# A ring of weights and its rounded copies, each 64 bytes off its former place modulo 128, in a split-fp32 transformer kernel

## What is computed

```
x = layer_norm(ALPHA * x + h, ...)
x = layer_norm(ALPHA * x + memory_cross_attention(x, mem, ...), ...)
x = layer_norm(ALPHA * x + conv_glu(x, ...), ...)
```

## The kernel before

| tile | lies on | start in bytes | modulo 128 |
|---|---|---|---|
| ring, w_lo | ring | 16512 | 0 |
| x_lo | tri | 80512 | 0 |
| s_lo | xt2 | 57472 | 0 |
| arena, h_hi, h_lo, m_hi, m_lo, s_hi, w_half, w_swo, yT | arena | 114624 and on | 64 |
| x_hi | arena + 4 x 18432 | 188352 | 64 |
| w_hi | arena + 4 x 20480 | 196544 | 64 |
| xlat, sc_in, small | own | 106432, 105280, 102336 | 64 |

## Time and profile before

### The profile page before, as it was taken

How to read it: one execution, slowest core, us unless ns; L and a number is a source line. 1 busy time by engine, 2 the same in 40 slices (tenths; PEclk the granted TensorE clock), 3 DMA queues, 4 the chain that set the end, 5 groups by cost and what they waited for, 6 DMA issues and landing times.

```text
span 2034.1 us, 33951 instructions
## 1 busy us (share of the span) xinstructions
PE 1919.6 (94%) x13633; PEld 1703.3 (84%) x13633; DVE 1077.8 (53%) x1502; ACT 996.0 (49%) x1703; POOL 1255.3 (62%) x585
## 2 busy tenths in 40 slices
PE   7989999999999989999998899999889999999997
PEld 7889798987999966879987787877679988959996
DVE  5472246633610073135557645688539943947971
ACT  4654345543444362436653444478645545535542
POOL 8758466687888503648896334100569886318995
PEclk9999999999999999999999899999999999988999
DMA  7335377774555534435552222344345554224552
GB/s 263 144 126 206 104 274 304 306 273 166 187 188 187 194 139 163 187 145 186 187 195 100 83 83 83 127 164 166 106 153 186 186 186 148 102 83 172 189 186 103
DMA packets 49218, 342.32 MB, mean 168 GB/s; under 512 B 5264, under 2 KB 7312, under 8 KB 8144
## 3 DMA queue, kind: packets, MB, share of 16 engines
q1 hardware_dynamic: 47440, 331.02, 45.1%
q0 software_dynamic: 1664, 9.70, 1.3%
HBM read 339.65 MB, written 1.05 MB: 167 GB/s over the span
## 4 chain that ended last, share of the span: by engine, by line
PE 73%; DVE 10%; POOL 6%; ACT 6%; issue 4%; DMA 1%; DVEq 0%; POOLq 0%; SPq 0%; ACTq 0%
PE bank L1831 13%; PE bank L1774 11%; PE bank L1768 11%; PE bank L1771 11%; POOL w_lo L2339 4%; PE bank L1881 3%; PE bank L1811 2%; PE bank L1809 2%; PE bank L1806 2%; PE bank L1353 2%; PE bank L1355 2%; PE bank L1356 2%; PE bank L1587 2%; DVE arena L765 2%; ACT arena L1181 1%
## 5 line engine op out<-in xcount | busy, mean ns | idle before, releaser
L2339 POOL TENSOR_TENSOR w_lo<-ring,w_hi 128x1024 fp32r<-128x1024 f32 x404 | 983.7, 2462 | 299.6 <-ACT w_hi L2949 281.4
L1768 PE MATMUL bank<-x_hi,w_hi 128*128 128x256 f32 x2176 | 613.9, 282 | 16.4 <-POOL w_lo L2339 13.0
L1774 PE MATMUL bank<-x_lo,w_hi 128*128 128x256 f32 x2176 | 619.1, 284 | 0.0
L2949 ACT ACTIVATE w_hi<-ring 128x1024 fp32r<-128x1024 f32 x448 | 448.8, 1052 | 293.4 <-DMA ring<-slabs_dram 284.1
L1771 PE MATMUL bank<-x_hi,w_lo 128*128 128x256 f32 x1824 | 511.5, 280 | 0.0
L1768 PEld LDWEIGHTS bank<-x_hi,w_hi 128*128 128x128 f32 x2176 | 414.6, 191 | 27.2 <-issue 27.2
L1774 PEld LDWEIGHTS bank<-x_lo,w_hi 128*128 128x128 f32 x2176 | 413.9, 190 | 0.0
L1771 PEld LDWEIGHTS bank<-x_hi,w_lo 128*128 128x128 f32 x1824 | 348.1, 191 | 0.0
L2871 ACT ACTIVATE arena<-bank 128x512 f32<-128x512 f32 (+1 forms) x179 | 98.3, 562 | 278.8 <-PE bank L1774 190.1
L458 POOL TENSOR_TENSOR w_lo<-ring,w_half 128x1024 fp32r<-128x1024 f32 x32 | 78.1, 2444 | 113.3 <-ACT w_half L1069 113.3
L2339 POOL TENSOR_TENSOR w_hi<-ring,w_hi 128x1024 fp32r<-128x1024 f32 x44 | 104.4, 2395 | 47.9 <-ACT w_hi L2949 47.9
(11 more groups left out here) (365 smaller groups left out, 3685.0 us busy)
## 6 DMA issues: line engine op xcount, KB each, us to landing
ring<-slabs_dram SPq DMA_DIRECT2D x308, 1024.0 KB, 4.8
lnrow<-ln_dram POOLq DMA_DIRECT2D x6, 1024.0 KB, 6.5
arena<-slabs_dram SPq DMA_DIRECT2D x4, 1024.0 KB, 8.0
xt<-xT_dram SPq DMA_DIRECT2D x1, 1024.0 KB, 5.7
xt<-memT_dram SPq DMA_DIRECT2D x1, 1024.0 KB, 11.8
x<-x_dram SPq DMA_DIRECT2D x1, 1024.0 KB, 13.6
arena<-ctx_dram POOLq DMA_DIRECT2D x1, 1024.0 KB, 7.1
lnrow<-ln_dram POOLq DMA_DIRECT2D x2, 512.0 KB, 4.7
```

Of the source, the lines that this page charges most:

```text
L1768: ins = pe.matmul(dst, wh[:, k, c], src[0][:, k, :], start=(k == 0 and (ch == 0 or not both)), stop=False, skip_group_check=both)
L1774: ins = pe.matmul(dst, wh[:, k, c], src[1][:, k, :], start=False, stop=(k == KC - 1), skip_group_check=both)
L2339: pool.tensor_tensor(dst[:, c], ring[:, s, c], w_hi[:, s, c].bitcast(F32), ALU.subtract).then_inc(S["lo_ready"], 1)
L2949: a.activation(w_hi[:, g % RING, c], ring[:, g % RING, c], ACT.Copy) \
```

## The change

Only declarations change. `tri`, `x` and `pt` come ahead of `ring`, `small` moves behind `arena` and is 16 elements shorter, `arena` is 16 elements longer, and `w_hi` starts 20496 elements into it instead of 20480. Three small tiles inside `small` move, one of them (`dcol`) onto `nmx`. The list of instructions of each engine, with its waits, is the same before and after.

```
+        tri_at = aligned()
+        tri = sb("tri", [P, 4, NT, T])
+        x = sb("x", [P, NT, D])
+        pt = sb("pt", [P, NPT])
         ring_at = aligned()
         ring = sb("ring", [P, RING, SLAB])
-        x = sb("x", [P, NT, D])
         xt2_at = aligned()
         xt2 = sb("xt2", [P, KC, 2 * T])
...
-        tri_at = aligned()
-        tri = sb("tri", [P, 4, NT, T])
         lnrow = sb("lnrow", [P, 2, D])
-        pt = sb("pt", [P, NPT])
         row = sb("row", [P, NROW])
-        small = sb("small", [P, 544])
...
-        arena = sb("arena", [P, 28672])
+        arena = sb("arena", [P, 28688])
+        small = sb("small", [P, 528])
...
-        pick = small[:, 256:288]
+        pick = small[:, 232:264]
...
-        dcol = small[:, 232:248]
+        dcol = small[:, 56:72]
...
-        w_hi = part("w_hi", arena_at + 4 * 20480, RING, SLAB)
+        w_hi = part("w_hi", arena_at + 4 * 20496, RING, SLAB)
```

More of the change, by code:

```diff
@@ L221, in aligned @@
             return -(-nc.sbuf_base // 32) * 32
+        tri_at = aligned()
+        tri = sb("tri", [P, 4, NT, T])
+        x = sb("x", [P, NT, D])
+        pt = sb("pt", [P, NPT])
         ring_at = aligned()
         ring = sb("ring", [P, RING, SLAB])
-        x = sb("x", [P, NT, D])
         xt2_at = aligned()
         xt2 = sb("xt2", [P, KC, 2 * T])
-        xT = xt2[:, :, T:2 * T]
-        sideT = xt2[:, :, 0:T]
         ident = sb("ident", [P, P])
@@ L243, in build @@
         arena_at = aligned()
-        arena = sb("arena", [P, 28672])
+        arena = sb("arena", [P, 28688])
+        small = sb("small", [P, 528])
+        xT = xt2[:, :, T:2 * T]
+        sideT = xt2[:, :, 0:T]
         def cut(at, *dims):
@@ L270, in build @@
         half16 = small[:, 136:152]
-        pick = small[:, 256:288]
+        pick = small[:, 232:264]
         modA = small[:, 168:184]
-        lamp = small[:, 288:416]
-        dtn = small[:, 288:544].rearrange("p (t h) -> p t h", t=4)
+        lamp = small[:, 264:392]
+        dtn = small[:, 264:520].rearrange("p (t h) -> p t h", t=4)
         sub_col = small[:, 230:231]
```

## The result

| | before | after |
|---|---|---|
| runs (median) | 2033.4 to 2035.92 us (2034.2, six runs) | 2041.6 to 2044.91 us (2042.56, six runs) |
| ratio of the medians, 95% interval | | 1.0043, 1.0033 to 1.0053 |
| profiled execution, span | 2036.21, 2034.1 us | 2042.38, 2040.3 us |
| granted clock | 0.974 | 0.976 |

The change costs 8.4 us.

The account below looks back on a forecast made before the run. The prediction took TensorE's pace, how fast matmuls follow each other, to bound the kernel. Its terms, +12.2 us for T on x against smaller gains, summed to +0.5 us: 2034.6 us against the median of 2034.16, range 2027 to 2041 us.

Parts of the forecast that it names:

- rival 4: Loads or GpSimd's remainders slow down at the new places and TensorE waits: 5 us or more; chance 0.04.
- T on x: Three-matmul split products on x outside net f0, 1824 triples: 53 steps for 52, 6.67 ns each, +12.2 us.
- One rule fits all five: At 256 columns, moving operand and next stationary operand: 18 steps of 6.67 ns if address / 64 has like parity, 17 if unlike.
- T in f0: The same form T in net f0, its remainder in a slot of w_hi, 352 triples: 52 steps for 53, -2.3 us.
- T on m: Form T with operand m, 8 slabs, 128 triples: two unlike pairs for one, -0.9 us.
- N on m: Form N, with w_hi and w_lo moving, on m, 128 triples: two unlike pairs for one, -0.9 us.
- R on h: 512-column matmuls in groups of six on h, 176 groups: 206 steps for 208, -2.3 us; bounds 0 and -4.7.
- N on x: Form N on x, 256 triples: 51 steps for 54, -5.1 us; bounds -3.4 us (52 steps) and -10.2 us (48).
- Form H: Triples of 512-column matmuls; s_lo and w_lo both move, three like-parity pairs as before: 0 us.
- swo: 8 slabs, 32 groups using w_swo and yT: six like-parity pairs for four, 210 steps for 208, +0.4 us.
- R on x: 512-column groups of six on x, 48 groups: -0.6 us, bounds 0 and -1.6; 3 steps of its old pace unexplained.
- Rival 1: TensorE pays in form T, N on x gives only -3.4 us, 512-column forms gain nothing: +5.1 us, 2039.3 us; chance 0.19.

Follow-up runs that it names:

- e3: The kernel before with `small` (2176 bytes) declared ahead of the ring, all tiles keeping their places modulo 128: 2043.51 us, ratio 1.0048.
- e2: The kernel after with `w_hi` back at 20480 elements into the arena, so that the ring alone is off its place: 2041.13 us, ratio 1.0039.
- e4: The kernel after with `small` moved from the end to between `ring` and `xt2`: 2018.28 us, ratio 0.9927.

## Why the prediction was wrong

- **What bounds the kernel: right.** The pace of matmuls that wait for nobody is what the addresses move. TensorE's first wait (13.1 us for 13.0), the DMA's share in both windows and a remainder's 2461 ns are as before (rival 4 is out), and the pace did change (rival 3 is out). The independence of loads and running matmuls in the Trainium skill ("TensorE: Matmul & The Clock Gate", Step-by-step: what each phase is for), which the prediction set aside, is contradicted once more where TensorE is alone: the same 24 matmuls of form H take 5.84 or 5.72 us by their addresses only.
- **T on x, +12.2 us: right in size**, 353.4 ns measured against 353.3. The reason given for it was wrong: e3 has the parities of before and runs at 353.3.
- **The step that failed is "One rule fits all five: a pair of unlike parity costs 17 steps, a pair of the same parity 18".** Five numbers of only three values, 52 to 54 steps, were fitted by a rule with two prices and a free choice of pairing, and every gain of the sum hung on it. The runs put in its place the distance modulo 256 bytes and a rhythm of the whole sequence: with all parities kept, e3 costs 9.4 us, and T on x goes from 346.7 to 353.3 ns. The table ahead of the prediction gave the places modulo 128 only, which hides half of it: x_lo and x_hi, which keep their places there, are 128 bytes closer or further modulo 256, since `small`, 2176 bytes, left its place ahead of the arena.
- **The gains that hung on the rule** did not come: T in f0 +0.7 us for -2.3, T on m 0 for -0.9, N on m +0.4 for -0.9, R on h +0.7 for -2.3. Together they are 8.2 us too good. N on x gained half of its price, 350.0 ns for the 340 taken, -2.5 for -5.1 us; its upper bound "52 steps, the lowest seen" was 346.7 and so too low as well.
- **Form H, costed at 0, gave 2.5 us, and swo gave 0.7 where +0.4 stood.** The rule's one price for "same", 35 steps or 233.3 ns, doesn't hold at 512 columns: distance 0 is the cheapest pair there (226.7 ns) and 128 costs 232.5. After the change all pairs of H and swo are at distance 0, and they run at 682.2 / 3 = 227.4 and 227.6 ns.
- **R on x** was the warning. It had the pairs of R on h by the rule and took 3 steps more in the trace, and the prediction wrote "3 steps that I can't explain" and kept the rule with 0.55. One row in eight that breaks a rule fitted to the other seven says that the rule is a fit.
- **Rival 1** named the right outcome, TensorE pays in form T and gets little back, at 2039.3 us; the measured 2042.56 is beyond it, since it still gave 4.1 us to f0 and the memory forms and 3.4 us to N on x. The chance of a slower result, 0.20, was too small for a sum of one price that a row showed (+12.2, and that in another form, N on m) and seven that the rule alone gave. That this one came out right is luck in part: it follows from a rule that e3 refutes.

What stays open: what in the memory makes distance modulo 256 count, and why 512 columns turn its order round; whether it is the moving operand against its own weights or against the next ones (single pairs don't part the two); what in the kernel picks the rhythm of a net; why f0 takes turns. The forms' sums against the first profile of before are, with H of 256 columns in it, +7.5 us for e3 with the span +7.7, but +6.8 for e2 with the span +3.0 and -20.6 for e4 with the span -18.3. The rest of e2 is the clock's for the most part: 102.6 us at 1.2 GHz for 109.1, worth up to 3.2 us. On line 1639 alone, 64 matmuls of one column, it shows as 8.2 us for 10.4; that stage ends at a granted clock of 0.97 in e2 (1786 to 1790 us) and of 0.50 in before. In e4 it is 106.5 us, which is little, and the 2.3 us by which its span shrinks less than its forms stay open.

## What to carry to other kernels

Where fp32r matmuls run back to back with a new stationary operand each (no other type was measured so), the addresses of operands in SBUF are a tuning parameter: here they are worth 24 us between two layouts of one program. Measure the few repeating sequences at all placements modulo 256 in a small kernel that does nothing else, weight them by their counts, and take the best placement whose pace doesn't depend on how it is begun; a layout changed for another reason has to be measured for this too. And a rule fitted to as many rows as it has choices is worth an experiment ahead of a forecast: a row that breaks it weighs more than those that it fits.

## What was not expected of the hardware

- fp32r matmuls of 256 columns with a new stationary operand each follow each other after 113.3 ns (340.0 a triple) to 121.1 ns (363.4), by the addresses, with no other engine at work; of 512 columns after 226.6 ns (1359.5 for six) to 233.9 ns (1403.5).
- The order of distances is not the same for the two sizes: distance 0 costs 120.0 ns at 256 columns, the most, and 226.7 at 512, the least.
- It is finer than 64 bytes: 112 bytes take 115.1 ns, 96 and 80 take 120.0.
- One sequence at one placement can run in two rhythms (353 and 360 ns, 353 and 358, in after's T on m 353 and 367) and can keep one for a whole net, some 120 us.
- The mean granted clock of one unchanged program differs from run to run, and its time with it: in 13 runs of before 2032.2 to 2032.9 us at 0.976 and 2034.9 to 2036.2 us at 0.974. Two profiles whose time at 1.2 GHz differs (109.1 and 101.1 us in the first pair here) differ by that too.
